# Block 0 of a hybrid decoder step: the first K tile is rounded earlier, the forget gate moves behind slot 2, the next rows' statistics move to slot 8

## The reference

```python
h = _rmsnorm(x, norm_w)
z = jnp.einsum('btd,dc->btc', h, w_in).astype(F32)
gq, gk, gv, gg, glr, rq, rk, rv, rg = _split_cols(z)
la = (jax.nn.log_sigmoid(glr @ gla_w2 + gla_b) / GLA_GATE_TAU).reshape(B, T, GLA_HEADS, GLA_DK)
q_b = _rope(rq.reshape(B, T, RET_HEADS, RET_DK), pos)
k_b = _rope(rk.reshape(B, T, RET_HEADS, RET_DK), pos) * (RET_DK ** -0.5)
...
o_a = o_a * rsqrt(mean(o_a * o_a) + EPS) * gla_norm_w;  o_a = o_a * silu(gg)
o_b = group_norm(o_b) * ret_norm_w + ret_norm_b;        o_b = o_b * silu(rg)
y = x + jnp.einsum('btc,cd->btd', concat([o_a, o_b]), w_out)
```

## Time and profile before

| | |
|---|---|
| median of 3 runs | 1684.18 us (1683.59 to 1684.27) |
| profiled execution, its own time | 1683.42 us |
| its span, first to last instruction | 1681.6 us |
| mean granted TensorE clock | 0.999 |
| TensorE busy | 1658.7 us, 99% of the span |
| VectorE / GpSimd / ScalarE busy | 994.5 / 837.9 / 613.8 us |
| chain that ended last | PE 96%, DMA 1%, DVE 1% |

### The profile page before, as it was taken

How to read it: one execution, slowest core, us unless ns; L and a number is a source line. 1 busy time by engine, 2 the same in 40 slices (tenths; PEclk the granted TensorE clock), 3 DMA queues, 4 the chain that set the end, 5 groups by cost and what they waited for, 6 DMA issues and landing times.

```text
span 1681.6 us, 26257 instructions
## 1 busy us (share of the span) xinstructions
PE 1658.7 (99%) x9898; PEld 1362.6 (81%) x9898; DVE 994.5 (59%) x2340; ACT 613.8 (37%) x1159; POOL 837.9 (50%) x661
## 2 busy tenths in 40 slices
PE   6999999999999999999999999999999999999998
PEld 4888878888788887888878888788887888878886
DVE  7733575856765375454755346757677464784453
ACT  4423344233342333433343233332334333343332
POOL 4445445554454544555444454556545455454545
PEclk9999999999999999999999999999999999999999
DMA  7534357653564444753546534478444753453624
GB/s 263 164 106 122 101 202 223 186 156 126 182 181 119 120 138 138 163 153 93 157 132 151 134 88 152 166 171 223 130 154 138 163 145 94 143 172 91 163 90 142
DMA packets 311902, 249.54 MB, mean 148 GB/s; under 512 B 218464, under 2 KB 220896, under 8 KB 311776
## 3 DMA queue, kind: packets, MB, share of 16 engines
q1 hardware_dynamic: 237904, 113.36, 25.6%
q10 hardware_dynamic: 73872, 134.51, 24.5%
HBM read 209.12 MB, written 38.67 MB: 147 GB/s over the span
## 4 chain that ended last, share of the span: by engine, by line
PE 96%; DMA 1%; DVE 1%; SPq 0%; issue 0%; ACT 0%; ACTq 0%; POOLq 0%; POOL 0%; DVEq 0%
PE bank L716 82%; PE bank L975 3%; PE bank L981 2%; PE bank L779 1%; PE bank L959 1%; PE bank L937 1%; PE bank L916 1%; PE bank L683 1%; PE bank L1007 1%; PE bank L920 1%; PE bank L737 1%; PE bank L992 0%; PE bank L789 0%; PE bank L895 0%; DMA w_stage<-in_w_slots 0%; DMA out_k_rows<-region 0%
## 5 line engine op out<-in xcount | busy, mean ns | idle before, releaser
L269 POOL TENSOR_TENSOR w_lo<-w_stage,w_hi 128x512 fp32r<-128x512 f32 x264 | 363.1, 1396 | 332.6 <-ACT w_hi L262 332.6
L716 PE MATMUL bank<-h_hi,w_hi 128*128 128x512 f32 x1024 | 408.0, 398 | 3.9 <-DVE h_lo L356 3.9
L716 PE MATMUL bank<-h_lo,w_hi 128*128 128x512 f32 x1024 | 399.8, 390 | 0.0
L716 PE MATMUL bank<-h_hi,w_lo 128*128 128x512 f32 x1024 | 399.4, 390 | 0.0
L269 POOL TENSOR_TENSOR w_lo<-ss,w_hi 128x512 fp32r<-128x512 f32 x164 | 219.3, 1358 | 224.6 <-ACT w_hi L262 224.6
L262 ACT ACTIVATE w_hi<-w_stage 128x512 fp32r<-128x512 f32 x264 | 152.7, 624 | 349.1 <-PE bank L716 315.1
L716 PEld LDWEIGHTS bank<-h_hi,w_hi 128*128 128x128 f32 x1024 | 192.4, 188 | 55.2 <-issue 7.6
L716 PEld LDWEIGHTS bank<-h_hi,w_lo 128*128 128x128 f32 x1024 | 192.5, 188 | 41.2
L716 PEld LDWEIGHTS bank<-h_lo,w_hi 128*128 128x128 f32 x1024 | 192.6, 188 | 37.1
L716 PE MATMUL bank<-w_hi,m_hi 128*128 128x512 f32 x512 | 202.9, 396 | 0.0
L716 PE MATMUL bank<-w_hi,h_hi 128*128 128x512 f32 x512 | 200.7, 392 | 0.0
(11 more groups left out here) (214 smaller groups left out, 2180.4 us busy)
## 6 DMA issues: line engine op xcount, KB each, us to landing
w_stage<-in_w_slots ACTq DMA_DIRECT2D x264, 256.0 KB, 3.2
ss<-in_w_slots ACTq DMA_DIRECT2D x164, 256.0 KB, 3.1
v_b<-in_w_slots ACTq DMA_DIRECT2D x84, 256.0 KB, 3.0
region<-in_x_prompt SPq DMA_DIRECT2D x32, 512.0 KB, 4.4
xn<-in_x_t SPq DMA_DIRECT2D x16, 512.0 KB, 4.8
out_k_rows<-region SPq DMA_DIRECT2D x32, 256.0 KB, 3.8
k_n<-out_k_rows SPq DMA_DIRECT2D x256, 32.0 KB, 2.7
out_o_rows<-region SPq DMA_DIRECT2D x32, 256.0 KB, 2.0
```

The costliest lines, as they stand in the source:

```text
L269: pool.tensor_tensor(w_lo[:, r, c], stage(h), w_hi[:, r, c].bitcast(f32), ALU.subtract).then_inc(lo_done, 1)
L716: i = pe.matmul(P[q][:, :], x, y, start=(s == 0 and kk == 0 and c == 0), stop=(s == 3 and kk == 1 and c == 2), skip_group_check=True)
```

## The change

Three things move in block 0, and some waits go with them.

- ScalarE rounds K tile 0 (`next_hi(act, 0, 0)`) between the two halves of slot 1's weights; the DMAs of halves 4 and 5 are issued behind K tile 1.
- TensorE's `hT_slot0` and the samples' gate move from behind slot 1 (and from inside slot 2) to the end of slot 2; `gate_expand` moves to slot 3, and ScalarE's and VectorE's parts of the gates one slot later (`late`). With it `sample_gate` of VectorE (`al`) moves from w = 4 to w = 5. `z_transposed` behind slot 6 gets a wait for `V_LA`, the samples' first projection one for `V_H`.
- VectorE's `next_stats` of block 0 moves from w = 2 to w = 8; GpSimd's `rstd` for it from w = 8 to w = 9. The samples' norm moves ahead by two K tiles, `gmask` behind `hs`.

```diff
@@ GpSimd
-                        if w == 8 and n < NBLK - 1:
+                        if w == (9 if n == 0 else 8) and n < NBLK - 1:
                             pool.wait_ge(xstat.sem, xstat.at(n + 1, 4))
@@ TensorE
-                        if kind == 0 and n > 0:
+                        if kind == 0:
                             sample_gate()
...
-                            if n == 0 and u == 0 and s == 1:
-                                if q == 0:
-                                    sample_transposed(0)
-                                if q == 1:
-                                    gate_expand()
-                                if q == 2:
-                                    sample_gate()
+                            if n == 0 and w == 2 and q == 0:
+                                sample_transposed(0)
+                            if n == 0 and w == 3 and q == 1:
+                                gate_expand()
...
                         if kind == 0 and u < 6 and s % 2 == 1:
                             if s == 1:
+                                if u == 0:
+                                    pe.wait_ge(s_v.sem, s_v.at(l, V_H))
...
-                            if w == 2:
+                            if w == 2 + int(n == 0):
                                 pe.wait_ge(lrs_sb.sem, lrs_sb.at(l, 1))
...
                             if w == 6:
+                                pe.wait_ge(s_v.sem, s_v.at(l, V_LA))
                                 z_transposed(X[:, 256:384], 0)
...
                             first_slot()
-                            hT_slot0()
                             continue
...
+                        if n == 0 and w == 2:
+                            hT_slot0()
@@ ScalarE
             split_hi(act, 0)
+            next_hi(act, 0, 0)
             split_hi(act, 1)
-            load_half(act, 4)
-            load_half(act, 5)
-            for k in range(KT):
+            for k in range(1, KT):
                 next_hi(act, 0, k)
+                if k == 1:
+                    load_half(act, 4)
+                    load_half(act, 5)
...
-                        if w == 2:
+                        if w == 2 + late:
                             act.wait_ge(lrs_ps.sem, lrs_ps.at(l, 1))
...
-                        if w == 3:
+                        if w == 3 + late:
                             act.wait_ge(gx_ps.sem, gx_ps.at(l, 1))
...
+                    late = int(n == 0)
                     for w in range(SLOTS):
 
-                        if w == (1 if n > 0 else 2):
-                            act.wait_ge(slot_used, n * SLOTS + (1 if n > 0 else 2) + RING)
+                        if w == (1 if n > 0 else 3):
+                            act.wait_ge(slot_used, n * SLOTS + w + RING)
...
-                        if w == 2:
+                        if w == 2 + late:
                             for hf, src in ((0, ATT), (1, OB)):
@@ VectorE
-                if k == 7:
+                if k == 5:
                     sample_norm(0)
-            vec.wait_ge(const_in, 96)
-            vec.tensor_scalar(gmask[:, :], rmask[:, 0:TOK], 0.0, None, ALU.is_gt)
...
-                            if w == 4:
+                            if w == 4 + late:
                                 sample_gate()
...
+                    late = int(n == 0)
                     if n == 0:
                         sample_start(l)
+                        vec.wait_ge(const_in, 96)
+                        vec.tensor_scalar(gmask[:, :], rmask[:, 0:TOK], 0.0, None, ALU.is_gt)
...
-                        if w in (3, 4):
-                            hf = w - 3
+                        if w in (3 + late, 4 + late):
+                            hf = w - 3 - late
...
-                        if w == (2 if n == 0 else 1) and n < NBLK - 1:
+                        if w == (8 if n == 0 else 1) and n < NBLK - 1:
                             next_stats(vec, n + 1)
```

More of the change, by code:

```diff
@@ L754, in unit_slot @@
                     def unit_slot(u, s):
+                        w = 4 * u + s + 1
                         first = n * HALVES + 2 * (4 * u + s)
```

## The result

| | before | after |
|---|---|---|
| median of the runs | 1683.88 us (6) | 1690.77 us (6) |
| ratio, 95% interval | | 1.0042 [1.0031, 1.0054] |
| span of the profiled execution | 1681.6 us | 1689.0 us |
| mean granted TensorE clock | 0.999 | 0.997 |

The change makes the kernel 6.9 us slower; 1691.1 was forecast, in a range of 1688.2 to 1693.4.

What follows compares the result with a forecast made beforehand. TensorE, busy 99% of the span, was taken as the bound. Start -0.7, slot 5 +0.7, wait for `al` +5.75 and clock +1.2 sum to +7.0 us: 1684.18 + 6.95 = 1691.1 us, range 1688.2 to 1693.4.

Steps and rivals of the forecast that it cites:

- The start: Program start to slot 2: TensorE starts 1.4 us earlier, but slot 2 waits for GpSimd's `w_lo`, leaving -0.7 us.
- Gate and slot 5: Block 0, slots 2 to 5: later gates delay VectorE's q copies, so slot 5 waits 0.7 us (0 to 1.3).
- The added wait: Line 809, behind slot 6: TensorE's transpose waits for `al`, now behind `rotate`, until 66.2 us: 5.75 us.
- main term: TensorE's wait at line 809 for `al` behind `rotate`, forecast at 5.75 us.
- TensorE's clock: Behind the wait at line 809: six products run at half rate, adding 1.2 us (0 to 2.5).
- Rival 1: Behind the wait at line 809 the clock stays up: 1689.9 to 1690.8 us; chance 0.27.
- Statistics at w = 8: TensorE's first outputs: scores ready at 85.5, 6.7 us wait alone, 0 to 0.9 behind the wait for `al`.
- second stall: TensorE's first outputs waiting for scores behind the moved statistics: 6.7 us alone, covered by the wait at line 809.
- Rival 3: First outputs: the statistics' wait lies on top, with k's trip 2 us later: +8.5 us, 1692.7; chance 0.10.
- rival 4: No wait at line 809, only the statistics' wait acts: +4.8 to +6.8, 1689 to 1691 us; chance 0.06.
- Rival 2: `rotate` slips between GpSimd's pairs, k tiles some 4 us earlier, not slower: 1684.2 us; chance 0.07.
- The signs: Profile marks: one 5 to 6.5 us wait at line 809; wrong if block 0 waits sum under 5 us more.

Runs made afterwards that it cites:

- experiment 1: Changed kernel with VectorE writing `al` ahead of the rotary work again, statistics still at w = 8: 1691.99 us, ratio 1.0049.
- experiment 2: Changed kernel with both put back, `al` ahead of the rotary work and statistics at w = 2: 1684.67 us, ratio 1.0005.
- experiment 5: Kernel before with only `al` moved behind the rotary work and TensorE waiting for it at line 809: 1690.02 us; second look, one execution, 1685.54 us.
- Experiment 4: Changed kernel with twenty unused products on TensorE ahead of its wait at line 809: 1689.16 us, ratio 1.0035.
- experiment 6: Kernel before with only block 0's statistics moved to w = 8 and GpSimd's rsqrt to w = 9: 1693.16 us, ratio 1.0053.
- experiment 8: Kernel before with only ScalarE's part of the program start changed, gates left behind slot 1: 1682.97 us, ratio 0.9995.
- experiment 9: Changed kernel with `al` and statistics put back, q banks copied ahead of the second gate half, GpSimd's rsqrt between slot 2's `w_lo`: 1682.26 us, ratio 0.9989.

## Why the prediction was right, step by step

- **The start**, forecast TensorE at 15.0 and slot 2 at 24.0, -0.7: measured 14.95 and 24.17, -0.57. The limit is GpSimd's `w_lo` pair, as said, with 1.3 us of wait where 1.7 was named as its sign; TensorE's clock rose one product later.
- **Gate and slot 5**, forecast first half at 41.5, copies at 47.6, wait 0.7: measured 41.51, 47.82, wait 1.12. The sum of both steps was to be 0, and is +0.32.
- **The added wait**, forecast 5.75: 5.11 - 0.32 = 4.8 arose there. Of the 0.95 too many, 0.55 is the end of `al`, at 65.50 in place of 66.05 (the rotary stretch with the copies took 17.5 us in place of 18.3, and began 0.2 later), 0.3 is TensorE, which came that much later, and 0.1 is the way from VectorE's end to TensorE, 0.06 us in place of 0.15. This was the main term, and experiments 1, 2 and 5 show its cause.
- **TensorE's clock**, forecast 1.2, bounds 0 to 2.5: 2.0. The term was too small because I took six slow products from the start, and there were nine, at a granted clock of 0.51; 2.0 lies within its bounds. Experiment 4 gives 1.8 us of the span back. Rival 1 falls. The idle array put back to half rate, which the Trainium skill states (TensorE: Matmul & The Clock Gate, "What's actually happening"), is what the windows show.
- **Statistics at w = 8**, forecast a second stall that the first covers: no wait at line 917. The scores were ready at 82.0 where I had 85.5, because I took two durations from the kernel before that GpSimd had disturbed, and neither was disturbed here: `keys` and the samples took 4.0 us in place of 5.9, the statistics 5.6 in place of 6.7; the other 0.55 is k, back at 71.62 and not at 72.2. That k's trip moves with `rotate`, as I said, experiment 6 contradicts. Covered the second stall is, but standing alone it costs as much as the first (experiments 1 and 6). Rival 3, a second stall on top of the first, falls with it. So does rival 4, since TensorE does wait at 809; its figure of 4.8 to 6.8 for the second stall alone was too small, since it left out the clock.
- **Not foreseen**: 0.3 us between the first outputs and the end, with one wait of 0.47 at line 938 in block 1, where k came back from its DMA trip later. The sum was 6.95, the medians differ by 6.9 us, the spans by 7.4. The mechanism is right, but that the number is this close is luck: the main term was 0.95 too high, the clock 0.8 and the start with slot 5 0.3 too low.
- **Rival 2** (the rotary work slips between GpSimd's pairs) was too far-fetched as stated, but part of it is real: in experiment 5 the stretch was 16.4 us in both looks, and in experiment 8 too. Its k tiles some 4 us earlier are not: in experiment 6 k's loops end 3 us earlier and k returns 0.2 us later than in the kernel before.
- **The signs.** Two of them just failed, though the account holds. The wait at 809 was to be 5 to 6.5 us, and is 4.73. TensorE's waits in block 0 were to sum to at least 5 us more than before, or I was wrong; they are 9.8 us (4.73 + 2.63 + 1.34 + 1.12) against 4.9 (3.92 + 0.96), so 4.9 more. Both limits were set too close to a main term that was 0.95 too high, and neither counts what the clock costs.
- **The range.** By the terms that it names, its lower end is 1684.18 + 4.75 = 1688.9 and not 1688.6, and its upper end, 1693.4, lies below the 1693.7 that it names. Neither touches the result.

## What to carry to other kernels

A semaphore wait on a tiny step costs what stands ahead of that step on its engine: before moving one, add up the stream ahead of it and compare that with the time at which the waiting engine arrives. When two waits lie in one stretch, test each alone, since the first hides the second, and mending only one gains nothing. A wait of some 5 us on TensorE cost 1.8 to 2.8 us more here through its clock.

## What the runs showed of the hardware that was not expected

- A wait of 2.80 us on TensorE lowered its clock in one execution and not in another of the same kernel (experiment 5: products 0.43 or 0.23 apart behind it). Waits of 4.7 to 6.0 us lowered it in all five profiles that have one, waits of 0.3 to 1.5 us behind slot 1 in none.
- The number of slow products at the start differs between executions: 6 in the kernel before, 7 in the changed one, 10 in experiment 8, 12 in experiment 9, at 0.2 us each. The granted clock of 10 to 20 us reads 1.00 in the kernel before all the same, while it reads 0.51 for the slow stretch at 65 us.
- Two copies of 64x16 took 0.36 us, and 1.39 us beside GpSimd's subtraction (experiment 1), 1.0 more; a rotary multiplication of 128x512 took 0.69 and 1.67, also 1.0 more.
- k's trip through DRAM, from the end of its rotary loops to its return, took 12.8 to 19.2 us in these kernels, and k was back between 70.7 and 74.2 us even where the loops ended 3 us earlier.
